# Two-layer decoder trunk on one core: merged products with the compressed keys and values, ScalarE's exponentials one step later, constants loaded later

## The reference

```python
# q of one head (256 tokens); per group of 6 heads: k_cmp, v_cmp: 15 compressed rows; ks, vs, kw, vw: 256 rows
s_c = q @ k_cmp.T * scale;  p_c = masked_softmax(s_c, c_end <= t)      # compressed branch
s_s = q @ ks.T * scale;     p_s = masked_softmax(s_s, causal)          # selected (with 4 blocks all are selected)
s_w = q @ kw.T * scale;     p_w = masked_softmax(s_w, causal)          # window
o = g0 * (p_c @ v_cmp) + g1 * (p_s @ vs) + g2 * (p_w @ vw)             # g: sigmoid gates of the head
# a memory head: softmax(q_mem @ km.T * scale) @ vm
```

## Time and profile before

| what | value |
|---|---|
| median of three runs | 2247.45 us |
| profiled execution, device time | 2249.05 us |
| its span (first to last instruction) | 2247.3 us |
| TensorE busy | 2232.0 us, 99% |
| VectorE busy | 1595.7 us, 71% |
| ScalarE busy | 1152.1 us, 51% |
| DMA traffic | 459 MB, mean 204 GB/s |

### The profile page before, as it was taken

How to read it: one execution, slowest core, us unless ns; L and a number is a source line. 1 busy time by engine, 2 the same in 40 slices (tenths; PEclk the granted TensorE clock), 3 DMA queues, 4 the chain that set the end, 5 groups by cost and what they waited for, 6 DMA issues and landing times.

```text
span 2247.3 us, 26491 instructions
## 1 busy us (share of the span) xinstructions
PE 2232.0 (99%) x10220; PEld 1845.4 (82%) x10220; DVE 1595.7 (71%) x2163; ACT 1152.1 (51%) x1558; POOL 18.7 (1%) x20
## 2 busy tenths in 40 slices
PE   9999999999999999999999999999999999999998
PEld 7888888888888888888888877788888888888887
DVE  6777675788878888544566667757888888885444
ACT  7556674655444544444574544446554444544443
POOL 0000000000000000000030000000000000000000
PEclk9999999999999999999999999999999999999999
DMA  9554556676777767676655843356777767766664
GB/s 321 181 170 152 187 169 197 198 235 222 236 234 223 232 228 234 197 230 190 197 179 182 267 132 99 117 174 201 238 230 231 237 217 238 236 217 201 193 195 150
DMA packets 128141, 459.00 MB, mean 204 GB/s; under 512 B 14768, under 2 KB 16816, under 8 KB 127248
## 3 DMA queue, kind: packets, MB, share of 16 engines
q1 hardware_dynamic: 127744, 456.78, 63.9%
q0 software_dynamic: 128, 0.48, 0.1%
q10 hardware_dynamic: 144, 0.05, 0.0%
HBM read 443.71 MB, written 2.10 MB: 198 GB/s over the span
## 4 chain that ended last, share of the span: by engine, by line
PE 94%; DVE 4%; ACT 1%; issue 0%; DMA 0%; SPq 0%; DVEq 0%; ACTq 0%
PE bank L577 93%; DVE lo L1188 1%; PE bank L700 0%; ACT hi L915 0%; DVE qm L1262 0%; DVE km L1262 0%; DVE ps L1500 0%; DMA raw<-in_mem 0%; PE bank L714 0%; ACT ps L1134 0%; DVE x L1314 0%; ACT ps L1130 0%; PE bank L747 0%; ACT psc L1130 0%; DVE st L1281 0%
## 5 line engine op out<-in xcount | busy, mean ns | idle before, releaser
L1188 DVE TENSOR_TENSOR lo<-raw,hi 128x1024 fp32r<-128x1024 f32 x776 | 945.5, 1223 | 528.8 <-ACT hi L915 522.3
L577 PE MATMUL bank<-hi,h 128*128 128x512 f32 x3904 | 1227.2, 392 | 0.4 <-ACT h L958 0.4
L915 ACT ACTIVATE hi<-raw 128x1024 fp32r<-128x1024 f32 x776 | 817.0, 1058 | 787.7 <-PE bank L577 766.1
L577 PEld LDWEIGHTS bank<-hi,h 128*128 128x128 f32 x3904 | 732.9, 188 | 152.3 <-issue 0.9
L577 PE MATMUL bank<-lo,h 128*128 128x512 f32 x1952 | 759.9, 389 | 0.0
L577 PE MATMUL bank<-hi,mid 128*128 128x512 f32 x1408 | 433.7, 389 | 0.0
L577 PEld LDWEIGHTS bank<-lo,h 128*128 128x128 f32 x1952 | 366.7, 188 | 74.0
L577 PEld LDWEIGHTS bank<-hi,mid 128*128 128x128 f32 x1408 | 264.3, 188 | 55.0
L577 PE MATMUL bank<-lo,mid 128*128 128x512 f32 x704 | 273.9, 389 | 0.0
L577 PE MATMUL bank<-hi,o 128*128 128x512 f32 x512 | 164.1, 394 | 0.0
L1425 DVE STREAM_TRANSPOSE cv<-mf 32x256 f32<-32x256 f32 x352 | 154.0, 437 | 6.4
(11 more groups left out here) (231 smaller groups left out, 1235.4 us busy)
## 6 DMA issues: line engine op xcount, KB each, us to landing
raw<-in_gate SPq DMA_DIRECT2D x176, 512.0 KB, 4.1
raw<-in_up SPq DMA_DIRECT2D x176, 512.0 KB, 3.6
raw<-in_down SPq DMA_DIRECT2D x176, 512.0 KB, 4.1
raw<-in_in SPq DMA_DIRECT2D x136, 512.0 KB, 4.2
raw<-in_out SPq DMA_DIRECT2D x64, 512.0 KB, 3.6
taps<-in_taps SPq DMA_DIRECT2D x44, 512.0 KB, 4.9
raw<-in_mem SPq DMA_DIRECT2D x31, 512.0 KB, 4.4
st<-st SPq DMA_DIRECT2D x22, 448.0 KB
```

The lines of the kernel that those rows point to most:

```text
L577: return mm(out, lhsT, rhs, start=first, stop=last, skip_group_check=True)
L915: act(hi[k][:, 0:w], raw[k][:, 0:w], ACT.Copy).then_inc(hi_done, 1)
L1188: tt(lo[k][:, 0:w], raw[k][:, 0:w], hi[k][:, 0:w].bitcast(F32), ALU.subtract).then_inc(lo_done, 1)
```

## The change

Three edits:

- **Products with the compressed rows.** The compressed keys now lie behind the keys in `kT`, so that the first tile's scores with 256 keys and 15 compressed keys are one product of 271 columns. In `nsaC` the compressed values take one product of 256 columns instead of two of 128, second in the order instead of last. For this `nsaB` transposes the compressed parts to the halves of bank 6, and the second tile's parts go to bank 7; there are eight transposes as before.
- **ScalarE's order.** For the memory heads of layer 1 and the sparse heads, ScalarE's part of the A step stands one tick later, behind the rounding of the next piece.
- **The start.** The first transfer of `memT` is cut in two of 128 KB, the second behind piece 0. `cst` and `msk` are issued when four pieces have been split.

```diff
-        do(t, "memA", 4 + g, on="pe act dve")
+        do(t, "memA", 4 + g, on="pe dve")
+        do(t + 1, "memA", 4 + g, on="act")
...
-        do(t, "nsaA", h, on="pe dve act")
+        do(t, "nsaA", h, on="pe dve")
+        do(t + 1, "nsaA", h, on="act")
...
-                    sp_.dma_start(memT[:, 0:2, :], A["memT"][:, 0:2, :]).then_inc(s_first_mem, 16)
+                    sp_.dma_start(memT[:, 0:1, :], A["memT"][:, 0:1, :]).then_inc(s_first_mem, 16)
                     sp_.dma_start(raw[0][:, W:2 * W], kv_piece(c, p)[:, W:2 * W]).then_inc(landed[0], 16)
+                    sp_.dma_start(memT[:, 1:2, :], A["memT"][:, 1:2, :]).then_inc(s_second_mem, 16)
...
 # nsaA, TensorE
-                add(S0[:, 0:T], q[0], kT[:, g, :, 0:P], True, False)
-                for t in range(2):
-                    add(S0[:, T + 16 * t:T + 16 * t + NC], q[t], kcmp[:, g, :], False, False)
+                add(S0[:, 0:T + NC], q[0], kT[:, g, 0, 0:T + NC], True, False)
+                add(S0[:, T + 16:T + 16 + NC], q[1], kT[:, g, 0, T:T + NC], False, False)
...
-                add(S1[:, :], q[1], kT[:, g, :, :].rearrange("p b t -> p (b t)"), True, False)
+                add(S1[:, :], q[1], kT[:, g, :, 0:T].rearrange("p k (b t) -> p b k t", b=2), True, False)
...
 # nsaC, TensorE
-                for b, pt in enumerate((pts, ptw)):
-                    at = slice((2 * b + g) * P, (2 * b + g + 1) * P)
-                    add(O[:, 0:T], v1[:, 0, at], pt[:, 0:T], b == 0, False)
-                    add(O[:, P:T], v1[:, 1, at], pt[:, T:T + P], False, False)
-                for b, pt in enumerate((pts, ptw)):
-                    m = add(O[:, half(b)], vcmp[0:NC, g, :], pt[0:NC, 3 * P:4 * P], False, b == 1)
-                m.then_inc(pv_ready, 1)
+                vs, vw = (slice((2 * b + g) * P, (2 * b + g + 1) * P) for b in range(2))
+                add(O[:, 0:T], v1[:, 0, vs], pts[:, 0:T], True, False)
+                add(O[:, 0:T], vcmp[0:NC, g, :], pts[0:NC, T:2 * T], False, False)
+                add(O[:, 0:T], v1[:, 0, vw], ptw[:, 0:T], False, False)
+                add(O[:, P:T], v1[:, 1, vs], ptw[:, T:T + P], False, False)
+                add(O[:, P:T], v1[:, 1, vw], ptw[:, T + P:2 * T], False).then_inc(pv_ready, 1)
...
+                act_.wait_ge(s_second_mem, 16)
                 act(amem[:, 1, 0, :], memT[:, 1, :], ACT.Copy, scale=gains[:, 0, 2, 1:2]).then_inc(mhi_done, 1)
...
+            pool.wait_ge(lo_done, 4)
             pool.dma_start(cst[:], A["consts"]).then_inc(s_small, 16)
             pool.dma_start(msk[:], A["masks"]).then_inc(s_small, 16)
```

More of the change, by code:

```diff
@@ L371, in build @@
         _, _, kT, kc, vc = region([
-            ("o_a", [P, DT, 2, T], F32R), ("q4_a", [P, 2, 4, T], F32), ("kT", [P, GROUPS, 2, T], F32),
+            ("o_a", [P, DT, 2, T], F32R), ("q4_a", [P, 2, 4, T], F32), ("kT", [P, GROUPS, 2, T + 16], F32),
             ("kc", [P, GROUPS, T], F32), ("vc", [P, GROUPS, T], F32)])
@@ L376, in build @@
             ("blkf0", [P, CMP_LEN, 2 * NC], F32), ("blkf1", [P, CMP_LEN, 2 * NC], F32), ("gt", [P, T], F32)])
-        common = [("km", [P, MEM_HEADS, T], F32), ("vm", [P, 2, W], F32), ("qm", [P, MEM_HEADS, T], F32),
+        common = [("gap", [P, 64], F32), ("km", [P, MEM_HEADS, T], F32), ("vm", [P, 2, W], F32), ("qm", [P, MEM_HEADS, T], F32),
                   ("pm", [P, 2, T], F32), ("ptm", [P, 2, T], F32)]
-        (amem, memT, km, vm, qm, pm, ptm, v4, ab, rl, sph, spl, aw, row0) = region(
+        (amem, memT, _, km, vm, qm, pm, ptm, v4, ab, rl, sph, spl, aw, row0) = region(
             [("amem", [P, DT, 2, T], F32R), ("memT", [P, DT, T], F32), *common, ("v4", [P, 2, 2, W], F32),
@@ L383, in build @@
         shadow = [("o_b", [P, DT, 2, T], F32R), ("memT_b", [P, DT, T], F32)] + [(n + "_b", s, d) for n, s, d in common]
-        (v1, cosf, sinf, ropeD, w2, pe, ps0, ps1, psc, pts, ptw, kcmp, G) = region(
+        (v1, cosf, sinf, ropeD, w2, pe, ps0, ps1, psc, pts, ptw, G) = region(
             shadow + [("v1", [P, 2, W], F32), ("cosf", [P, 2, P], F32), ("sinf", [P, 2, P], F32),
@@ L388, in build @@
                       ("psc", [P, 2, 16], F32), ("pts", [P, W], F32), ("ptw", [P, W], F32),
-                      ("kcmp", [P, GROUPS, NC], F32), ("G", [P, HEADS, 6], F32)])[len(shadow):]
+                      ("G", [P, HEADS, 6], F32)])[len(shadow):]
         row2, = region(shadow + [("v1_c", [P, 2, W], F32), ("row2", [P, D], F32)])[len(shadow) + 1:]
@@ L434, in build @@
         s_mem = [sem(f"s_mem{q}") for q in range(4)]
-        s_first, s_first_mem, warm_set = sem("s_first"), sem("s_first_mem"), sem("warm_set")
+        s_first, s_first_mem, s_second_mem, warm_set = (sem(n) for n in ("s_first", "s_first_mem", "s_second_mem", "warm_set"))
         first_whi, first_wlo, first_mhi, first_mlo = (sem(n) for n in ("first_whi", "first_wlo", "first_mhi", "first_mlo"))
@@ L837, in nsaB @@
                 pe_.wait_ge(np_ready, hd + 1)
[L838 to L844, removed]
+                take(6, npt_act, hd + 1)
+                for t in range(2):
+                    tr(B[6][0:NC, T + t * P:T + (t + 1) * P], psc[:, t, 0:NC], ident)
+                tr(B[6][:, 0:P], ps0[:, 0, :], ident)
+                tr(B[6][:, P:T], ps1[:, 0, 0:P], ident).then_inc(nt_ready, 1)
+                take(7, npt_dve, hd + 1)
+                tr(B[7][:, 0:P], ps0[:, 1, :], ident)
+                tr(B[7][:, P:T], ps1[:, 1, 0:P], ident)
+                for b in range(2):
+                    m = tr(B[7][:, T + b * P:T + (b + 1) * P], ps1[:, b, P:T], ident)
+                m.then_inc(nt_ready, 1)
             def nsaC(hd):
@@ L1245, in turned_copy @@
                     two = slice(2 * i, 2 * i + 2)
-                    to = {"km": km[:, two, :], "qm": qm[:, two, :], "kcvc": (kc, vc)[i][:], "kskw": kT[:, :, i, :]}.get(dest)
+                    if dest == "kskw":
+                        copy(kT[:, :, :, i * P:(i + 1) * P], B[b][:].rearrange("p (g k t) -> p g k t", g=GROUPS, k=2))\
+                            .then_inc(copied, 1)
+                        continue
+                    to = {"km": km[:, two, :], "qm": qm[:, two, :], "kcvc": (kc, vc)[i][:]}.get(dest)
                     if to is None:
@@ L1477, in cmp @@
                 if k == 0:
-                    copy(kcmp[:].rearrange("p g c -> p (g c)"), B[6][:, 0:2 * NC]).then_inc(cmp_done, 1)
+                    copy(kT[:, :, 0, T:T + NC], B[6][:, 0:2 * NC].rearrange("p (g c) -> p g c", g=GROUPS)).then_inc(cmp_done, 1)
                 else:
```

## The result

The changed kernel takes 2256.72 us (median of six runs, 2256.15 to 2257.84) against 2247.84 us of the kernel before in the same comparison: a ratio of 1.004, 95% interval 1.003 to 1.0051, 8.9 us slower. Forecast were 2253.8 us, and a range of 2249 to 2257.

A forecast was written before the change was run, and what follows sets the result against it. TensorE was taken to bound the kernel, busy 2232.0 of 2247.3 us. Terms -3.2 - 2.4 - 0.4 + 7.9 + 4.5 = +6.4 us took the median neighbour from 2247.45 to 2253.85, rounded to 2253.8; range 2249 to 2257.

The forecast's parts named there:

- ScalarE's order at three places: Memory head 1, sparse heads 1 and 5: exponentials queue behind an evacuation, TensorE stands 2.75, 2.75 and 2.4 us more; 7.9 lost.
- The clock: Behind the three new TensorE stalls: a stretch at 1.2 GHz follows each, 1.5 us apiece, 4.5 us lost.
- a longer stall than the first must bring it: Clock argument: the 2.1 us start stall was followed by half clock, so stalls of 2.75, 2.75 and 3.4 us are too.
- The start: Up to piece 2: constants and part of memT issued later, TensorE begins piece 2 at 12.65 instead of 15.84; 3.2 us saved.
- what is late next: piece 2: Step at the start: after piece 0's second half, piece 2 is late next; its rounding starts at 9.7, activations' rest ends at 12.65.
- Merged products: A and C of twelve heads: two fewer records of 15 columns save 0.20 us a head in A, C nothing; 2.4 saved.
- happens once before and once now: In C: the change to 15-row weights and back, 0.28 us, stays one per head, so C was taken at 0.
- Head 0: Transposes at head 0: VectorE's late `lo` comes earlier, so the longest wait there goes; 0.4 us saved.
- the ten other heads at nothing: ScalarE's order at ten heads: the rounding of 1.05 us fits in 1.52 us of idle time before the exponentials; nothing gained.
- The rule on the least distance of two starts: Merged products in A: by near 25 ns they save only 0.3 us, the sum 2.1 higher; the trace's 0.112 was preferred.

The follow-up runs named there:

- Experiment 1: The changed kernel with ScalarE's exponentials ahead of an evacuation at the same tick; 2245.26 us, ratio 0.999.
- experiment 2: The kernel before with only ScalarE's part of the layer 1 heads' A steps one tick later; 2259.58 us, ratio 1.0054.
- experiment 9: The changed kernel with exponentials ahead of the evacuation at the sparse heads only, memory head 1 left behind it; 2249.4 us, ratio 1.0005.
- experiment 4: The changed kernel with 24 useless products ahead of the wait for bank 4 at C of heads 0 and 4; 2255.04 us, ratio 1.0032.
- experiment 3: The changed kernel with ScalarE's order of before, keeping the new start and products; 2246.17 us, ratio 0.9994.
- experiment 5: The kernel before with only the constants issued behind the fourth split; 2246.31 us, ratio 0.9994.
- experiments 10 and 11: The first of Experiments 7 and 8 with VectorE's rotations ahead of a memory head's maxima, 2242.14 us; then also memT's first transfer in one again, 2241.5 us.
- experiment 6: The kernel before with only memT's first transfer cut in two, the second part behind piece 0; 2248.66 us, ratio 1.0006.
- Experiments 7 and 8: Experiment 1 with C's 15-row product last: as one of 256 columns, 2243.4 us; with C's six products of before, two of 128 columns last, 2243.26 us.

## Why the prediction was nearly right, by its own steps

- **ScalarE's order at three places (+7.9).** Right in place, cause and size. Two waits of 2.6 us on `ps` and one of 3.3 at the turning; 5.6 + 2.4 = 8.0 in the shifts. Experiment 1 takes them away by the order alone, experiment 2 makes them on the kernel before, experiment 9 isolates the third.
- **The clock (+4.5).** The mechanism was right as far as tested: in experiment 4 TensorE has work in two of the stalls, C starts as late as before, and the half clock behind them is absent. The size of one fall was right (1.6 against 1.5). Where it comes was not: the shorter stalls were followed by it in this profile and the longest was not. In experiments 4 and 9 the wait at the turning, as long, was followed by it; in experiment 2 it was not, one stall gave a double stretch and the next none. My argument that a longer stall than the first must bring it is not what the traces show; it comes after most such stalls, not after each.
- **The start (-3.2).** The term was too large, for two reasons. The first is a step left out: "what is late next: piece 2" skips piece 1. TensorE can't start piece 2 before it has done piece 1, which waited for its own `lo` until 10.66 and takes 2.85 us; 13.51 follows, and the trace gives 2.3 us. The later landing of the second half (rounded at 6.5, not 5.3) does not decide this, as experiment 3 shows. The chain of piece 2 itself was reckoned short as well: its rounding began at 10.23 instead of 9.7, and even from 9.7, with the distances of the earlier trace rows (2.23 from rounding to the activations' rest, then 0.87), it ends at 12.8 and not at 12.65. The second reason is that I took the half clock in the one profile of before for what every execution has. Against the start of experiment 2's profile, which lacks it (piece 2 at 14.13), the start gives 0.6 us, and the constants alone give 1.25 in the medians (experiment 5). That is most of the step from 2253.8 to 2256.7: with 0.6 in place of 2.3, the table sums to 8.8, and the medians differ by 8.9. I had also put the cut of `memT` on the side of the gain; it costs 0.6 us (experiments 10 and 11) to 1.1 (experiment 6).
- **Merged products (-2.4).** A's saving is there: 0.60 us from A's first product to the masks against 0.80 before, 0.2 a head. C's sum of time stayed, as reckoned. What failed is the step that took C at nothing because the change back from 15-row weights "happens once before and once now". It moved ahead of C's last product, from a place beside VectorE's chain to one on it, and TensorE waits 0.2 us at each B for it. Experiments 7 and 8 give that back, whether the products are merged or not. I had bounded C's cost by up to 0.2 a head, but for a further change of weights, not for its place. In experiment 1, which has no stalls, the products are worth 1.0 us in the shifts; the 1.5 of the table has 0.4 more, since B finds no such wait behind the two stalls.
- **Head 0 (-0.4), and the ten other heads at nothing.** Right: the step at head 0 is there in every kernel with the new order and not in experiment 3.
- The rule on the least distance of two starts (the Trainium skill, "TensorE: Matmul & The Clock Gate", section "Wait — 56ns, not 53.3ns?", near 25 ns) would by the prediction's estimate have made the merging worth 0.3 us. The trace has such a distance only at the first record of 15 columns (0.029 us to the next); the others keep 0.11 us, and two records less in A save 0.2 us a head, 2.4 in all.
- That the time lies within the range owes something to luck: the start was 2.6 us too good and the merged products 0.9, and the clock, 1.2 too dear, took a part of that back.

Open is what decides whether the clock falls behind a given stall; the same kernel shows both. The executions at 2255.0 and 2253.0 of experiment 4 are told apart by that only by argument.

## What to carry to other kernels

When a step moves by one tick on an in-order engine, list what else has its place on the new tick, and ask of each what it waits for: here an evacuation that waits for the end of a product stood ahead of exponentials that the next product waited for, and the rank of ScalarE's exponentials was worth 11.5 us. Where a chain on another engine hangs on the last product of a group, the costly change of weights belongs behind that product; merging products that stream the same columns gained nothing here, while dropping records of 15 columns did. When a load comes earlier, follow every piece from there on in order: the next to be late was the one that the reckoning skipped. And a single profile can hold an event that most executions do not have: compare its span with those of the timed runs before an estimate rests on it.

## What the runs showed of the hardware that I had not expected

- Behind the eight unfilled stalls of 2.6 to 3.3 us in these profiles (three in the changed kernel, three in experiment 2, one each in experiments 4 and 9) the granted clock fell from 2.4 to 1.2 GHz five times, four times for 3.4 us and once for 6.8 (experiment 2). Of three stalls of 1.9 to 2.0 us at the start (the kernel before, experiments 6 and 7) it fell behind one, that of the kernel before. A fall of 3.4 us cost 1.5 to 1.6 us. Behind the two filled stalls of experiment 4 it did not come.
- Between products with weights of 15 rows and of 128 rows there is a gap of 0.2 us each way: in the changed kernel's C, records of 256 columns start 0.31, 0.32, 0.30 and 0.32 us apart around the product of 15 rows, and 0.216 elsewhere, so each way spreads over two distances.
- A 128x512 moving operand read in four strided chunks of 128 took the same 0.51 + 0.43 us in its two records as the contiguous one before.
